# Second feed-forward: squaring, rounding and splitting the inner tiles by quadrants of 512 tokens

## The reference, cut to what matters

```python
h = jnp.square(jax.nn.relu(x @ w_up[layer]))
x = layer_norm(DN_ALPHA * x + h @ w_down[layer], ln_ffn_g[layer], ln_ffn_b[layer])
```

## Time and profile before

| | us |
|---|---|
| median of 3 runs | 3033.5 (3030.36 to 3033.65) |
| the profiled execution's own time | 3034.26 |
| its span, first to last instruction | 3032.5 |
| TensorE busy | 2846.9 (94%) |
| VectorE busy | 1777.0 (59%) |
| GpSimd busy | 1301.6 (43%) |
| ScalarE busy | 886.3 (29%) |
| mean granted TensorE clock | 0.972 of full |

### The profile page before, as it was taken

The page is one execution under the profiler, slowest core; times in us unless marked ns, Lnnn a source line. Parts: engine busy times, 40 slices in busy tenths (PEclk is TensorE's granted clock), DMA queues, the critical chain, the costliest instruction groups (busy, mean ns, idle before and its releaser), DMA issues.

```text
span 3032.5 us, 35019 instructions
## 1 busy us (share of the span) xinstructions
PE 2846.9 (94%) x12838; PEld 2293.7 (76%) x12838; DVE 1777.0 (59%) x2338; ACT 886.3 (29%) x1604; POOL 1301.6 (43%) x765
## 2 busy tenths in 40 slices
PE   7989999999998999999999799999898999999997
PEld 4767777886776888888887677888675787777774
DVE  3888999888635333333234548888757533433337
ACT  3442301118413111111112446666513211112223
POOL 2432334441332333333334325555542655556661
PEclk9989999999999999999999999999898999999998
DMA  3211112221321111111111200000111111111111
GB/s 144 59 35 35 42 63 77 81 78 49 134 89 35 49 49 49 48 48 48 48 44 54 112 15 29 22 29 22 59 53 35 35 56 49 48 55 48 48 47 64
DMA packets 44736, 165.78 MB, mean 55 GB/s; under 512 B 5000, under 2 KB 5640, under 8 KB 43600
## 3 DMA queue, kind: packets, MB, share of 16 engines
q1 hardware_dynamic: 36448, 128.85, 12.8%
q10 hardware_dynamic: 8176, 35.43, 3.1%
HBM read 146.66 MB, written 16.78 MB: 54 GB/s over the span
## 4 chain that ended last, share of the span: by engine, by line
PE 75%; DVE 18%; issue 3%; ACT 3%; DVEq 1%; POOL 1%; DMA 0%; ACTq 0%; SPq 0%; POOLq 0%
PE dense L671 16%; PE dense L672 16%; PE dense L675 16%; PE side L1232 2%; PE side L1234 2%; PE side L1233 2%; PE dense L1105 2%; PE dense L1106 2%; PE dense L1107 2%; DVE stay L2450 2%; DVE a_lo L1969 2%; PE dense L711 1%; DVE T L2576 1%; PE dense L712 1%; PE dense L713 1%
## 5 line engine op out<-in xcount | busy, mean ns | idle before, releaser
L515 POOL TENSOR_TENSOR w_hi<-raw,zero 128x1024 fp32r<-128x1024 f32 x154 | 300.3, 1950 | 1146.1 <-PE dense L675 877.3
L671 PE MATMUL dense<-a_hi,w_hi 128*128 128x512 f32 x1552 | 611.1, 394 | 22.0 <-DVE gates L2209 9.8
L672 PE MATMUL dense<-a_lo,w_hi 128*128 128x512 f32 x1552 | 607.1, 391 | 0.0
L675 PE MATMUL dense<-a_hi,w_lo 128*128 128x512 f32 x1552 | 480.1, 391 | 0.0
L517 POOL TENSOR_TENSOR w_lo<-raw,w_hi 128x1024 fp32r<-128x1024 f32 x154 | 396.1, 2572 | 12.1
L671 PEld LDWEIGHTS dense<-a_hi,w_hi 128*128 128x128 f32 x1552 | 293.5, 189 | 88.7 <-issue 10.0
L671 PE MATMUL dense<-b_hi,w_hi 128*128 128x512 f32 x832 | 328.8, 395 | 11.4 <-DVE b_lo L2578 6.4
L675 PEld LDWEIGHTS dense<-a_hi,w_lo 128*128 128x128 f32 x1552 | 292.8, 189 | 61.6
L672 PEld LDWEIGHTS dense<-a_lo,w_hi 128*128 128x128 f32 x1552 | 293.6, 189 | 59.8
L672 PE MATMUL dense<-b_lo,w_hi 128*128 128x512 f32 x832 | 325.0, 391 | 0.0
L2336 DVE TENSOR_TENSOR x_res<-x_res,dense 128x1024 f32<-128x1024 f32 x100 | 122.1, 1221 | 314.4 <-PE dense L675 313.7
(11 more groups left out here) (326 smaller groups left out, 5498.2 us busy)
## 6 DMA issues: line engine op xcount, KB each, us to landing
raw<-in_w_stream SPq DMA_DIRECT2D x231, 512.0 KB, 3.4
x_in<-in_x_t SPq DMA_DIRECT2D x8, 512.0 KB, 7.3
spill_gate<-T ACTq DMA_DIRECT2D x8, 512.0 KB, 2.6
spill_part<-gates ACTq DMA_DIRECT2D x8, 512.0 KB, 2.6
back<-spill_gate ACTq DMA_DIRECT2D x8, 512.0 KB, 3.7
back<-spill_part ACTq DMA_DIRECT2D x8, 512.0 KB, 4.6
x_res<-in_x_t ACTq DMA_DIRECT2D x2, 2048.0 KB, 8.8
spill_x<-x_res ACTq DMA_DIRECT2D x1, 4096.0 KB, 13.8
```

What stands on the lines that cost most here:

```text
L515: pool.tensor_tensor(w_hi[:, r % 2, :], raw[:, r, :], zero[:, 0:1].broadcast_to([P, D]), ALU.add).then_inc(weights_rounded, 1)
L671: pe.matmul(o, w_hi[:, slot, w], hi[:, k, x], start=b == 0, stop=False)
L672: pe.matmul(o, w_hi[:, slot, w], lo[:, k, x], start=False, stop=False)
L675: last = pe.matmul(o, w_lo[:, slot, w], hi[:, k, x], start=False, stop=stop)
```

## The change

The order of the four quadrants of a pair gets a name, `QUADS`: (0, first half), (1, second half), (0, second half), (1, first half), which is the order in which they are finished.

- VectorE: instead of three sums and then two squares and two low parts of 1024 tokens, it does for each quadrant in this order: the sum (for the first three), a drain, the square of 512 tokens, the wait for ScalarE's high part, the low part of 512 tokens. The numbers of sums and elements are as before; squares and low parts are four of 512 each in a pair, not two of 1024.
- ScalarE: four `hidden_high` of 512 tokens in a pair, not two of 1024. Their places: the first quadrant's after piece 5 and before copy 1, the second's after copy 2 (for c = 0 after piece 0 of the next pair and before its piece 1), the third's right before copy 3, and the fourth's in the next pair between pieces 2 and 3, or at the end of the group. Copy 3 applies the relu itself (`ACT.Relu` for `ACT.Copy`).
- The semaphores `squared` and both of `parts["hidden2"]` count 8 quadrants for a group, not 4 tiles. TensorE waits in the down projection for all 4 quadrants of the first pair, then for the third quadrant of the second pair ahead of block 2, and for the fourth ahead of block 3.

```diff
--- before.py
+++ after.py
@@ -306,6 +306,8 @@
         t1, t2 = (at(f"t{n}", [P, 4, 512], F32, Y0 + kib) for n, kib in ((1, 78), (2, 94)))
         t3, t3_end, t4 = at("t3", [P, 3, 512], F32, Y0 + 32), at("t3_end", [P, 512], F32, 105), at("t4", [P, 4, S], F32, 56)
 
+        QUADS = ((0, 0), (1, 1), (0, 1), (1, 0))
+
         def low_half(q):
             return slice(0, 512) if q % 2 == 0 else slice(512, 1024)
 
@@ -601,7 +603,7 @@
                 for n in range(2):
                     pool.wait_ge(weights_loaded[(t + n) % RAW], i * (16 * FF2_TILES // 2) + (16 * ((t + n) // 2) + 16))
                 if c == 0:
-                    pool.wait_ge(parts["hidden2"][1], i * FG)
+                    pool.wait_ge(parts["hidden2"][1], i * 8 - 4)
                 pool.tensor_tensor(w_sum, w21, w22, ALU.add).then_inc(w_combined, 1)
                 pool.wait_ge(piece_rounded, i * 10 + (5 * pair + 1))
                 lower(0, w11).then_inc(piece_split, 1)
@@ -1251,11 +1253,11 @@
                     else:
                         pe.wait_ge(weights_split, i * FF2_TILES + (t + 1))
                     if m == 0:
-                        pe.wait_ge(hidden, i * FG + (FG - 2))
+                        pe.wait_ge(hidden, i * 8)
                         product(t % 2, halves(dense, u % 2), b_hi, b_lo, FG - 2, 0, end=False)
-                        pe.wait_ge(hidden, i * FG + (FG - 1))
+                        pe.wait_ge(hidden, i * 8 + 3)
                     product(t % 2, halves(dense, u % 2), b_hi, b_lo, FG - 1, m * FG, begin=0 if m else FG - 2, end=False)
-                pe.wait_ge(hidden, i * FG + FG)
+                pe.wait_ge(hidden, i * 8 + 4)
                 for m in range(2):
                     product(t % 2, halves(dense, (U_DOWN2 + m) % 2), b_hi, b_lo, FG, m * FG, begin=FG - 1
                             ).then_inc(tile_done if m else first_done, 1)
@@ -1829,33 +1831,37 @@
                                    ).then_inc(part_copied, 1)
                 else:
                     act.wait_ge(tile_done, i * FF2_TILES + (t + 2))
-                    act.wait_ge(parts["hidden2"][1], i * FG + 2 * c)
-                    act.activation(T[:, 1, 0:512], quad_bank(3 * c), ACT.Copy).then_inc(part_copied, 1)
+                    act.wait_ge(parts["hidden2"][1], i * 8 + (4 * c - 4))
+                    act.activation(T[:, 1, 0:512], quad_bank(3 * c), ACT.Relu).then_inc(part_copied, 1)
 
             def sevenths(i):
-                def hidden_high(f):
-                    act.wait_ge(squared, i * FG + (f + 1))
-                    act.activation(b_hi[:, f, :], T[:, f % 2, :], ACT.Copy).then_inc(parts["hidden2"][0], 1)
+                def hidden_high(c, n):
+                    f, half = QUADS[n]
+                    act.wait_ge(squared, i * 8 + (4 * c + n - 3))
+                    act.activation(b_hi[:, 2 * c + f, cols(half)], T[:, f, cols(half)], ACT.Copy).then_inc(parts["hidden2"][0], 1)
 
                 round_piece(i, 0, 0)
                 round_piece(i, 0, 1)
                 for c in range(2):
                     round_piece(i, c, 2)
+                    if c:
+                        hidden_high(0, 3)
                     round_piece(i, c, 3)
-                    if c:
-                        hidden_high(1)
                     copy_part(i, c, 0)
                     round_piece(i, c, 4)
                     round_piece(i, c, 5)
+                    hidden_high(c, 0)
                     copy_part(i, c, 1)
                     round_piece(i, c, 6)
                     copy_part(i, c, 2)
                     if c == 0:
                         round_piece(i, 1, 0)
+                    hidden_high(c, 1)
+                    if c == 0:
                         round_piece(i, 1, 1)
-                    hidden_high(2 * c)
+                    hidden_high(c, 2)
                     copy_part(i, c, 3)
-                hidden_high(FG - 1)
+                hidden_high(1, 3)
 
             sevenths(1)
             with act.Fori(2, FF2_GROUPS - 1) as i:
@@ -2559,23 +2565,20 @@
             def sevenths(i, behind=None):
                 for c in range(2):
                     pair = c - 2
-                    dve.wait_ge(piece_done, i * 12 + (6 * pair + 2))
-                    dve.wait_ge(part_copied, i * 8 + (4 * pair + 1))
-                    dve.wait_ge(parts["hidden2"][1], i * FG + 2 * c)
-                    dve.tensor_tensor(T[:, 0, 0:512], quad_bank(1), first_copy, ALU.add).then_inc(quad_taken, 1)
-                    dve.wait_ge(piece_done, i * 12 + (6 * pair + 5))
-                    dve.wait_ge(part_copied, i * 8 + (4 * pair + 3))
-                    dve.tensor_tensor(T[:, 1, 512:S], quad_bank(3 * c), third_copy, ALU.add).then_inc(quad_taken, 1)
-                    dve.wait_ge(piece_done, i * 12 + (6 * pair + 6))
-                    dve.tensor_tensor(T[:, 0, 512:S], quad_bank(2), second_copy, ALU.add).then_inc(quad_taken, 1)
-                    dve.drain()
-                    for n in range(2):
-                        f = 2 * c + n
-                        if n:
+                    dve.wait_ge(parts["hidden2"][1], i * 8 + (4 * c - 4))
+                    for n, (f, half) in enumerate(QUADS):
+                        place = T[:, f, cols(half)]
+                        if n < 3:
+                            dve.wait_ge(piece_done, i * 12 + (6 * pair + (2, 5, 6)[n]))
+                            dve.wait_ge(part_copied, i * 8 + (4 * pair + (1, 3, 3)[n]))
+                            dve.tensor_tensor(place, quad_bank((1, 3 * c, 2)[n]), (first_copy, third_copy, second_copy)[n], ALU.add
+                                              ).then_inc(quad_taken, 1)
+                            dve.drain()
+                        else:
                             dve.wait_ge(part_copied, i * 8 + (4 * pair + 4))
-                        dve.scalar_tensor_tensor(T[:, n, :], T[:, n, :], 0.0, T[:, n, :], ALU.max, ALU.mult).then_inc(squared, 1)
-                        dve.wait_ge(parts["hidden2"][0], i * FG + (f + 1))
-                        dve.tensor_tensor(b_lo[:, f, :], T[:, n, :], b_hi[:, f, :].bitcast(F32), ALU.subtract
+                        dve.scalar_tensor_tensor(place, place, 0.0, place, ALU.max, ALU.mult).then_inc(squared, 1)
+                        dve.wait_ge(parts["hidden2"][0], i * 8 + (4 * c + n - 3))
+                        dve.tensor_tensor(b_lo[:, 2 * c + f, cols(half)], place, b_hi[:, 2 * c + f, cols(half)].bitcast(F32), ALU.subtract
                                           ).then_inc(parts["hidden2"][1], 1)
                 down(i, T_FF2 + FG, U_DOWN2, FF2_TILES, 12 + FULL * KB // 2 + KB // 2, behind,
                      tiles=KB // 2 if behind is not None else KB)
```

## The result

The changed kernel takes 3016.27 us (median of 5 runs, 3015.53 to 3017.04) for 3033.65 before (5 runs, 3030.36 to 3036.06): a ratio of 0.9942, 95% interval 0.9928 to 0.9957. The forecast was 3017.6, between 3012.5 and 3026.5. The profiled execution's span is 3014.8 us.

What follows compares the result with a forecast made beforehand. TensorE, busy 94%, was taken as the bound, with two waits a group to shorten. 7 x (0.6 + 1.44) = 14.3 us plus 1.6 for the clock, 15.9 in all, gave 3017.6 us; 8-in-10 range 3012.5 to 3026.5.

Steps and rivals of the forecast that it cites:

- The waits that went: TensorE, each group: q = 2 of the second pair waiting for ScalarE's copy, block 2 for `b_lo`; both were to go.
- The end of the pair: Down projection behind pair 1: third quadrant done ahead of block 2, fourth ahead of block 3; 1.44 us gained a group.
- the list laid out from the rows: Engines' instruction times laid out from profile rows; at pair 1's end, third quadrant done at 2521.5, fourth by about 2526.6.
- What is late next: Pair 0 to pair 1: GpSimd's weight pieces, q = 1 waiting for piece 1 until 2503.0, q = 2 for piece 2 until 2505.96.
- The term of 0.6 us: Pair 0 to pair 1: q = 3 starts at 2508.8 instead of 2509.38, 0.6 us gained of 2.56 lost there.
- L605's delay of 0.35: First quadrant's rounding ahead of copy 1 delays it some 0.35 us, moving L605 from 2494.06 to 2494.4; bounds 0 to 0.5.
- The turns: VectorE and GpSimd take turns: 512 tokens take 0.54 us after waiting, 0.69 alone; a GpSimd piece 1.15 or 1.29.
- the 0.4 that I had: Mean wait in us of each short VectorE instruction for GpSimd, in the forecast's list.
- rival "turns": Each short VectorE instruction waits out a whole GpSimd piece of 1.29 us; 10.5 us slower, 3044; chance 0.09.
- about 1.3: Sign on VectorE after the change: squares and low parts take 0.69 to about 1.3 us.
- The relu: Copy 3 on ScalarE: relu for Copy adds no table load, 0 us; a table load there would show the forecast wrong.
- The clock: Stretch from q = 2 to block 2: one of two slow-clock groups lost, 1.6 us gained; bounds 0 and 3.3.

Runs made afterwards that it cites:

- longer wait: Changed kernel plus one GpSimd instruction in the second pair, remaking 128 columns of weight piece 1's low part; 3025.94 us, 0.9974 of the kernel before.
- piece 1 early: Changed kernel with GpSimd making weight piece 1's low part right behind piece 0's, ahead of two differences; 3028.04 us, 0.9969 of the kernel before.
- second pair only: Changed kernel with quadrants for the second pair alone, the first pair by whole tiles as before; 3029.12 us, 0.9977 of the kernel before.
- ScalarE's old order: Changed kernel's quadrants on VectorE, but ScalarE rounds them at the places of its old list; 3027.45 us, 0.9978 of the kernel before.

## Why the prediction was right

**The waits that went.** Both did in all seven groups. The end of the pair was put at 1.44 us a group, and is 1.44: from the start of the down projection to the next group's q = 5 of the first pair it takes 57.4 us for 58.9 before. The third quadrant's low part ends 6.7 us behind the start of q = 5 (2519.79 for 2513.11), which is where the list laid out from the rows had it (2521.5 for 2514.8). The fourth ends 11.8 behind, also as laid out.

**What is late next.** GpSimd, as forecast: q = 1 was put 1.6 us behind its undisturbed start, and is 1.66 (2501.87 for 2500.21); q = 3 was put 10.14 behind q = 0 and comes at 10.17. The term of 0.6 us is 0.55. L605's delay of 0.35 is 0.4. With the 1.99 in sum for 2.04, these terms give 14 us for 14.3. That the time of the whole then shows it so well is in part luck: outside the groups the two profiled executions differ by 1.1 us one way and 1.1 the other, for no reason that was forecast.

**The turns.** From `w_sum` to the end of piece 2 GpSimd's list takes 11.40 us, for 11.92 before, though it now passes six short VectorE instructions and not three long ones. Squares and low parts took 0.69 to 1.77 in the first pair, mostly 1.0 and 1.10 on average over its eight: 0.56 above the 0.54 of the work itself, for the 0.4 that I had and the 1.0 from which the rival "turns" would have held. The longest are above the "about 1.3" that I named as a sign. The rival wants 1.8 each; of those shown, three took that or more (2498.84, 2519.71, 2522.79). The last two fall into slack. The first one touches a wait of TensorE's: the low part of piece 1 (2500.02) stands behind this square, takes 1.71 us, and ends the wait before q = 1. By the rule of the Trainium skill (SBUF — State Buffer, "Who interferes with whom") issue order decides, and the trace agrees: 2493.12 was first and took 0.69, L607 had to wait and took 1.67 for 1.29.

**The relu.** The trace after has no table load at copy 3 (11 in the whole kernel, as before).

**The clock: the right sign, too small.** I counted on 1.6 us, one fall of two. The profiled execution has no fall in seven groups, which is 3.3 us. The wait that I argued from, 1.3, doesn't follow from my own list either: q = 1 at 2503.0 is 1.6 behind its undisturbed 2501.38, and 1.3 is only what is added to the 0.3 of before. The wait came out at 1.50, and the clock didn't fall behind it. Kernels whose wait stays near 1.9 us show what would have come else: four falls with the longer wait, six with piece 1 early. This step was argued from two of seven groups. So the forecast of this term was right in its sign and half in its size, and there was not much room: the longest wait after, 1.50, is 0.3 us short of the shortest that a fall followed in any run (1.77). The sum was 15.9, the ratio gives 17.6 (13 to 22).

## What to carry to other kernels

When results come out in parts at different times, treat each part as it comes only if the engines that pass it on have their lists in the same order: with ScalarE's old list the same quadrants on VectorE kept well under half of the gain (0.9978 for 0.9942). Before moving work, lay out the lists of all engines from the trace's own durations; what becomes late next (here GpSimd's weight pieces) is seen in them, to a tenth of a microsecond in the prediction and to 0.2 or 0.3 in the later expectations of where q = 2 starts. And look at the longest single wait of TensorE, not only their sum: moving one weight piece ahead put off the start of q = 2 by 0.2 us only, but made a wait of 1.5 us one of 1.9, and cost 8 to 12 us in all.

## What was not expected of the hardware

In these kernels' groups the granted clock fell from 2.4 to 1.2 GHz behind single waits of TensorE of 1.8 us and more, in some groups and not in others: two of seven before (waits of 1.8 to 2.0), three of seven with the second pair only (1.9 to 2.0), six of seven with piece 1 early (1.8 to 1.95), four of seven with the longer wait (1.94 to 2.10), three of seven with ScalarE's old order (3.1 to 3.5). In group 4 of before, for one, the granted clock is 0.50 from 2680.24 to 2682.80, and the matmuls start 0.427 us apart in place of 0.227. It fell in none of the seven in the five kernels whose longest waits are 0.8 to 1.5 us, nor in the one with 1.8 in one group and 1.3 to 1.5 in the others. A fall costs 1.4 to 1.7 us from one group to the next.

Of two waits alike to 0.01 us one was followed by it and the other not, four waits of 3.1 to 3.3 us and one of 2.5 weren't followed by it either, so more than the wait decides it; what, these runs leave open. It is also the likely reason for the spread of the kernel before, 3027.8 to 3038.6 in all its runs, where the changed kernel has 3015.5 to 3017.0. The mean clock of the single runs goes that way: of those of before beside the experiments, all under 3032 us have 0.973 or 0.974, and twelve of the fourteen above 3037 have 0.972. Where in these runs it fell was not shown, as only one execution of each kernel was profiled.
